# Turned probabilities in the first two attentions of a diffusion block kernel: values behind turns, four homes instead of two

## The reference

```
p = softmax([q_b . k_window, q_b . k_ctx, sink])          # 8 heads of 64, two key heads
o_b = p_win @ v_b + p_ctx @ v_bc
s = q_c . [k_c, k_ctx] for 2 maps of each of 4 heads
pd = softmax(s[0]) - lam * softmax(s[1])                   # one matrix per head
o_c = pd @ [v_c, v_cc];  out_c = rms_norm(o_c, c_subln) * (1 - lam_init)
x = x + g1 * ([out_a, o_b, out_c] @ w_out)
x = x + g2 * conv_ffn(...)
```

## Time and profile before

| | us |
|---|---|
| three runs | 1609.86, 1599.04, 1604.06 |
| median of the three | 1604.06 |
| span of the profiled execution | 1602.1 |
| median less that span | 1.96 |
| PE busy in the span | 1533.7 (96%) |
| DVE, ACT busy | 1092.5 (68%), 839.3 (52%) |
| first attention on PE | about 160 to 240 |
| second attention on PE | about 742 to 787 |

### The profile page before, as it was taken

The page is one execution under the profiler, slowest core; times in us unless marked ns, Lnnn a source line. Parts: engine busy times, 40 slices in busy tenths (PEclk is TensorE's granted clock), DMA queues, the critical chain, the costliest instruction groups (busy, mean ns, idle before and its releaser), DMA issues.

```text
span 1602.1 us, 27276 instructions
## 1 busy us (share of the span) xinstructions
PE 1533.7 (96%) x9500; PEld 1278.7 (80%) x9500; DVE 1092.5 (68%) x1930; ACT 839.3 (52%) x1526; POOL 108.3 (7%) x170
## 2 busy tenths in 40 slices
PE   4999989999999999899899999999999999799997
PEld 2777667688888888897789997998788887588886
DVE  4444874797786477776678876654678855778865
ACT  3432873544444322465656665536566644566653
POOL 0111000110100011020000000020000000000000
PEclk9999999999999999999999999999899999799999
DMA  9766105565642488452167655541746587446663
GB/s 369 275 227 199 46 2 210 200 223 194 200 127 80 163 263 281 134 150 82 36 261 267 187 150 154 177 163 48 289 146 185 176 301 273 178 130 181 179 182 115
DMA packets 79685, 288.60 MB, mean 180 GB/s; under 512 B 9280, under 2 KB 12864, under 8 KB 71664
## 3 DMA queue, kind: packets, MB, share of 16 engines
q1 hardware_dynamic: 61056, 190.23, 37.7%
q0 software_dynamic: 18544, 97.23, 17.0%
HBM read 283.49 MB, written 1.05 MB: 178 GB/s over the span
## 4 chain that ended last, share of the span: by engine, by line
PE 69%; DVE 15%; issue 5%; ACT 5%; DMA 4%; DVEq 1%; ACTq 0%; SPq 0%; POOL 0%
PE B L1962 15%; PE B L1963 15%; PE B L1964 15%; DVE WLO L1205 6%; PE B L1979 4%; DMA RAW<-in_wdn 3%; PE B L1999 3%; PE B L1977 2%; DVE Y L1679 2%; PE B L2253 2%; ACT WHI L718 2%; DVE Y L1692 1%; PE B L1991 1%; PE B L1992 1%; PE B L1993 1%
## 5 line engine op out<-in xcount | busy, mean ns | idle before, releaser
L1205 DVE TENSOR_TENSOR WLO<-RAW,WHI 128x1024 fp32r<-128x1024 f32 (+1 forms) x376 | 411.5, 1099 | 151.8 <-ACT WHI L718 147.5
L718 ACT ACTIVATE WHI<-RAW 128x1024 fp32r<-128x1024 f32 (+1 forms) x376 | 357.2, 957 | 140.1 <-PE B L1964 86.6
L1962 PE MATMUL B<-HHL,WHI 128*128 128x256 f32 (+1 forms) x1184 | 397.3, 336 | 10.4 <-DVE HHL L1314 4.2
L1964 PE MATMUL B<-HHL,WLO 128*128 128x256 f32 (+1 forms) x1184 | 391.4, 331 | 0.0
L1963 PE MATMUL B<-HHL,WHI 128*128 128x256 f32 (+1 forms) x1184 | 391.3, 330 | 0.0
L1962 PEld LDWEIGHTS B<-HHL,WHI 128*128 128x128 f32 x1184 | 224.7, 190 | 44.4 <-issue 17.4
L1979 PE MATMUL B<-HHL,WHI 128*128 128x512 f32 x704 | 245.3, 401 | 1.7 <-DVE HHL L1314 1.7
L1964 PEld LDWEIGHTS B<-HHL,WLO 128*128 128x128 f32 x1184 | 224.9, 190 | 20.8
L1963 PEld LDWEIGHTS B<-HHL,WHI 128*128 128x128 f32 x1184 | 224.9, 190 | 19.8
L1977 PE MATMUL B<-HHL,WLO 128*128 128x256 f32 x704 | 184.6, 282 | 0.0
L1979 PE MATMUL B<-MID,WHI 128*128 128x512 f32 x462 | 163.8, 401 | 4.4 <-DVE WLO L1205 3.4
(11 more groups left out here) (264 smaller groups left out, 2215.6 us busy)
## 6 DMA issues: line engine op xcount, KB each, us to landing
RAW<-in_wup SPq DMA_DIRECT2D x176, 512.0 KB, 3.7
GWR<-in_wmod POOLq DMA_DIRECT2D x27, 1024.0 KB, 7.8
RAW<-in_wdn SPq DMA_DIRECT2D x64, 384.0 KB, 3.5
RAW<-in_wproj SPq DMA_DIRECT2D x44, 512.0 KB, 4.3
RAW<-in_wdn SPq DMA_DIRECT2D x64, 320.0 KB, 3.3
WDU<-in_wdot POOLq DMA_DIRECT2D x32, 512.0 KB, 4.9
WDD<-in_wdot POOLq DMA_DIRECT2D x32, 512.0 KB, 4.9
GWA<-in_wmod POOLq DMA_DIRECT2D x15, 1024.0 KB, 5.4
```

The lines of the kernel that those rows point to most:

```text
L718: act_f(WH[s][:, 0:kts, :], RAW[s][:, 0:kts, :], ACT.Copy).then_inc(hi_done, 1)
L1205: v.tensor_tensor(WL[s][:, 0:kts, :], RAW[s][:, 0:kts, :], WH[s][:, 0:kts, :].bitcast(F32), ALU.subtract).then_inc(lo_done, 1)
L1962: mm(bank[:, 0:t], wh, a, start=first and k == ks[0], stop=False)
L1964: ins = mm(bank[:, 0:t], wl, a, start=False, stop=stop and k == ks[-1])
```

## The change

In the step loop of PE, `turns(S[j - 2])` now stands ahead of `values(S[j - 3])`. Probabilities of layers 0 and 1 have four homes, in turn PTS half 0, PTS half 1, PTR half 0, PTR half 1 (PTR is a new tile in memory that is free during the attention); the copy of item i waits for the values of item i - 4 instead of i - 2. Layer 2 keeps two homes and its order. The two banks that the turns go to, the four score banks and PB are as before. Later lines of the file stand 8 lower.

```
+        PTR = sb("PTR", [P, 2, 512], at=w0 + 38912)
+        PT = [PTS[:, 0], PTS[:, 1], PTR[:, 0], PTR[:, 1]]
...
+        def turned(l, i):
+            return PT[i % 4] if IS_L[l] else PT[i % 2]
...
             def copy_pt(l, i, nk):
                 act.wait_ge(pt_mm, total(NITEM, l) + i + 1)
-                if i >= 2:
-                    act.wait_ge(pv_mm, total(NITEM, l) + i - 1)
-                act_f(PTS[:, i % 2, 0:nk], banks[2 + i % 2][:, 0:nk], ACT.Copy).then_inc(pt_ev, 1)
+                homes = 4 if IS_L[l] else 2
+                if i >= homes:
+                    act.wait_ge(pv_mm, total(NITEM, l) + i + 1 - homes)
+                act_f(turned(l, i)[:, 0:nk], banks[2 + i % 2][:, 0:nk], ACT.Copy).then_inc(pt_ev, 1)
...
                     if j < len(S):
                         scores(S[j])
-                    if j >= 3:
-                        values(S[j - 3])
                     if 2 <= j < len(S) + 2:
                         if j >= 11 and j % 8 == 3:
                             pe.wait_ge(rbs_ev, total([4, 2], l) + j // 8)
                         turns(S[j - 2])
+                    if j >= 3:
+                        values(S[j - 3])
```

More of the change, by code:

```diff
@@ L2307, in values @@
                                 ins = mm(OB["b"][64 * e:64 * e + 64, c:c + P], s["vals"][e][a // P + k],
-                                         PTS[:, i % 2, P * k:P * k + P], start=k == 0, stop=k == (b - a) // P - 1)
+                                         turned(l, i)[:, P * k:P * k + P], start=k == 0, stop=k == (b - a) // P - 1)
                         ins.then_inc(pv_mm, 2)
@@ L2313, in values @@
                         for k in range((b - a) // P):
-                            ins = mm(OB[s["kind"]][:, c:c + 64], PTS[:, i % 2, P * k:P * k + P], vals[a // P + k],
+                            ins = mm(OB[s["kind"]][:, c:c + 64], turned(l, i)[:, P * k:P * k + P], vals[a // P + k],
                                      start=k == 0, stop=k == (b - a) // P - 1)
@@ L2400, in values @@
                     for k in range(4):
-                        ins = mm(OBANK[it["grp"] % 2][:, c:c + P], PTS[:, i % 2, P * k:P * k + P], it["val"](k),
+                        ins = mm(OBANK[it["grp"] % 2][:, c:c + P], turned(l, i)[:, P * k:P * k + P], it["val"](k),
                                  start=k == 0, stop=k == 3)
```

## The result

The changed kernel takes 1609.04 us, median of 9 runs (1605.35 to 1613.68), the kernel before 1602.96 us on the same chip (1598.93 to 1609.86): a ratio of 1.0038 with a 95% interval from 1.0024 to 1.0053. It is slower by 0.4%. The span went from 1602.1 to 1608.3 us.

A forecast was written before the change was run, and what follows sets the result against it. PE was taken to bound the kernel, its waits paid in full. 0.05 + 2.75 + 3.77 + 2.4 - 1.1 - 0.4 = 7.5 us took the span from 1602.1 to 1609.6; with 1.96 to the median, 1611.5 us, range 1601 to 1618.

The forecast's parts named there:

- What bounds: Whole kernel: PE is busy 96% of the span, so its waits in the two attentions are paid in full.
- What is removed: PE's b values waiting for probability copies: at most 0.23 us per 512-key pair, plus larger waits at the ends.
- the ends: Last steps of each attention, up to the last turn of the sums: layer 1 -1.1 us, layer 0 -0.4.
- first rival: Combination is in time, only copy waits go (2.7 us layer 0, 2.3 layer 1): 1599.1; chance 0.12, whole or 512-key only.
- the loop: Each pair's period becomes DVE chain + 0.05 + c turn + b values: plain 512-key pairs 5.67 us.
- What is added: The c turn, uncovered, waits for DVE's combination in every pair: +2.75 and +3.77 us in layer 0, +2.4 in layer 1.
- lateness of DVE: Some 0.1 to 0.2 us in the extras of single pairs that can vanish when PE comes later: -1.
- unknown price of the new neighbours on PE: Changes of matmul shape in the new order, over some 20 pairs: -2 to +2 us, taken as zero.
- The total: Both attentions +7.5 us, span 1602.1 to 1609.6, time 1611.5 with 1.96 from span to median.
- The homes: Four homes for probabilities cost nothing and gain nothing themselves; they let PE's order change.
- Second rival: ACT joins the loop through later c copies: a further 0.4 us in some 19 pairs, 1619; chance 0.09.
- Third rival: PE's clock falls in the seven 256-key pairs: some 14 us more, 1625; chance 0.02.

The follow-up runs named there:

- e8: Changed kernel without the joining of the two maps (line 1493 left out) and with PE's old order, four homes kept: 1602.00 us, ratio 0.9994 to the kernel before.
- e3: Changed kernel without the joining of the two maps (line 1493 left out), new order and four homes kept: 1592.78 us, ratio 0.9939 to the kernel before.
- e4: Changed kernel with turns ahead of values in odd steps only, four homes: 1597.96 us, ratio 0.9971 to the kernel before.
- e1: Changed kernel with PE's old order (values ahead of turns), four homes kept: 1603.99 us, ratio 1.0000 to the kernel before.
- e2: Changed kernel with the two old homes, new order kept: 1617.39 us, ratio 1.0085 to the kernel before.
- e6: Changed kernel with turns ahead of values in odd steps only and the two old homes: 1603.00 us, ratio 1.0004 to the kernel before.
- e5: Changed kernel with the combination ahead of the b minima in DVE's step: 1619.08 us, ratio 1.0111 to the kernel before.
- e7: Changed kernel with DVE's combination straight behind the b minima, ahead of sum reciprocals and mixed-row split: 1604.03 us, ratio 1.0011 to the kernel before.

## Why the prediction was right

- **What bounds.** Right. PE bounds the stage, and each of its waits is paid: the stage grew by 6.85, the median by 6.1.
- **What is removed.** Right in kind, wrong in size. The waits for copies went in full, and the ends became shorter by 0.40 and 1.23 us against 0.4 and 1.1. But "the most that can be won is those 0.23 in each such pair" is the step that failed: pairs without a marked wait had one too, and marked ones a longer one. With the combination out of the way a pair of 512 keys falls from 5.63 or 5.47 to 5.27, and the order is worth 7.9 us (e8 against e3), where PE's list has 6.2, of which the first rival counts 5. This did not show in the total, since the loop hides it: what the period holds is the chain, the c turn and the b values, and the three of them were measured right.
- **What is added.** Right, and nearly to the digit: plain pairs 5.67 for 5.67, and all three bodies of pairs within 0.24 us of the sum. In layer 1 the pair with the reciprocals stands in the sum as 6.9, though the same kind has 7.03 in layer 0; it measured 6.92. The waits for the combination, 17.1 us, are longer than the 7 to 15 that I named as a sign, since PE had more time to spare than its list of waits showed. I had named up to 1 us for lateness of DVE that would vanish; 0.5 us of the bodies went that way or another. The unknown price of the new neighbours on PE, put at zero with 2 us to both sides, was near zero: with no wait in either, a pair takes 5.27 in the new order (e3) and 5.28 in e4's mixture. That matmuls with all operands ready stay behind a waiting one, on which the whole loop rests, the changed profile shows: the copies of the b values ended at 175.73, the turn ahead of them started at 176.32 and they at 176.90.
- **The total.** 1611.5 for 1609.04. Of the 2.5 us between them 0.6 are the stage, 0.65 what lies outside it, and 1.2 the offset from span to median: I added 1.96, and here the median lies 0.7 above the profiled span. With nine runs that of the kernel before (1602.96) lies 0.9 above its span.
- **The homes.** That they are no gain of their own is right for the old order (e1). That they are what lets the order change is wrong for the pairs, which take the same time with two (e2); only the ends pay. In e4's order they carry most of the gain (e4 against e6).
- **First rival** (the combination is in time). Refuted by the 22 waits. Its time was too high as well, for the reason above: 1599.1, where e3, the case without any combination, took 1592.8.
- **Second rival** (ACT in the loop). Not in the changed kernel: PE's list has no wait of a turn or a score for ACT there. It is what e5 brought about.
- **Third rival** (the clock). Not in the changed kernel's profile, which has 1.00 all through both attentions. But in e2, e5 and e7, which have similar waits, the clock did fall in the part with 256 keys. Its price was too high, since the clock was back after 3.4 us in e5 and e7, at about 1 us in e7, and not low over seven pairs. Whether it fell in some of the timed runs of the changed kernel isn't known.

## What to carry to other kernels

Work that an engine does between asking for something and needing it is cover for everything that is late at that point, not only for the wait that one looks at. Before moving it, measure the chain of the other engines that ends behind it (here 4.00 us from b scores to the joined probabilities) against what the engine has left to do in the meantime (3.8). In a loop of steps of two kinds, decide the order for each kind apart: the reversal paid in odd steps and cost in even ones, and with two more lines and one changed condition it gave -0.3% in place of +0.4%. And look for waits on the weight loads as well as on the matmuls: a short wait can be missing from the matmul's own row.

## What was not expected of the hardware

The clock can fall in or right behind a stretch with many short waits. In e2 PE was busy for 3.2 to 3.9 of each 5 us from 225 to 245, with no single wait over 1.2 us in the stage, and the granted clock then was 0.50 from 244.9 to 251.7, mostly while PE was back at full work. In e5 it was 0.50 from 244.5 to 247.9, after 3.3 to 4.0 us busy of each 5 from 220 to 240, and in e7 from 231.6 to 235.0, after 4.2 to 4.4 of each 5 from 215 to 230 and a wait of 1.09. The Trainium skill ("TensorE: Matmul & The Clock Gate", section "A second HAM failure mode: psum-queue depth-cycling") describes short idle times between groups of matmuls that do this. The three falls fit that, but no run here changes the waits alone to show it, and the changed kernel, with 3.4 to 3.9 of 5 us in the same stretch and waits as long, stayed at 1.00 in its profiled execution.
